# A fused Fourier and retention layer on one core: retention products, operand sums and gate buffers around the folded Fourier projection in another order

## The reference

```python
h_x = modulate(rms_norm(x, norm1_gain), sh1, sc1)            # sh1, sc1, g1, ... from silu(c) @ w_ada + b_ada
u, q, k, v, g, ga, gb = split(h_x @ w_in)                    # u is 512 wide: the Fourier branch
o      = bidirectional_retention(rope(q), rope(k), v)        # 8 heads of 64, chunks of 128
y_four = real(fft2(u over tokens and 128 channels, ortho)) @ four_w_out
y_ret  = (silu(g) * group_norm(o) * gn_gain) @ ret_w_out
y      = sigmoid(ga) * y_four + sigmoid(gb) * y_ret
x      = x + g1 * (y @ w_out)
x      = x + g2 * (square(relu(modulate(rms_norm(x)) @ w_mlp1)) @ w_mlp2)
out    = rms_norm(x) * final_gain
```

## Time and profile before

| | us |
|---|---|
| median of 3 runs (1300.51 to 1301.29) | 1301.24 |
| the profiled execution, its own time | 1299.87 |
| its span, first to last instruction | 1298.1 |
| PE busy | 1257.0 (97%) |
| DVE busy | 888.1 (68%) |
| ACT busy | 610.9 (47%) |
| POOL busy | 156.6 (12%) |

### The profile page before, as it was taken

How to read it: one execution, slowest core, us unless ns; L and a number is a source line. 1 busy time by engine, 2 the same in 40 slices (tenths; PEclk the granted TensorE clock), 3 DMA queues, 4 the chain that set the end, 5 groups by cost and what they waited for, 6 DMA issues and landing times.

```text
span 1298.1 us, 16931 instructions
## 1 busy us (share of the span) xinstructions
PE 1257.0 (97%) x6216; PEld 1037.9 (80%) x6216; DVE 888.1 (68%) x1392; ACT 610.9 (47%) x1038; POOL 156.6 (12%) x99
## 2 busy tenths in 40 slices
PE   6999999996999899999999999999999999999997
PEld 3788788885988688888888888888888888888886
DVE  5572587747556988878588766655646669868966
ACT  7761211244234443442668655555555433554544
POOL 0125420142141000015530000000000000000000
PEclk9999999998999899999999999999999999999999
DMA  9414220112157355567841544444438996468534
GB/s 368 170 33 154 81 91 2 33 23 94 44 175 253 122 198 201 210 250 271 325 160 66 194 152 160 151 160 141 162 114 283 315 287 211 161 220 266 191 101 163
DMA packets 95226, 219.18 MB, mean 169 GB/s; under 512 B 11532, under 2 KB 11932, under 8 KB 95144
## 3 DMA queue, kind: packets, MB, share of 16 engines
q1 hardware_dynamic: 84480, 188.99, 42.5%
q10 hardware_dynamic: 8872, 22.81, 4.8%
q0 software_dynamic: 1792, 6.29, 1.4%
HBM read 166.66 MB, written 51.39 MB: 168 GB/s over the span
## 4 chain that ended last, share of the span: by engine, by line
PE 62%; DVE 2%; issue 1%; DMA 0%; ACT 0%; ACTq 0%; DVEq 0%
PE ps L2975 9%; PE ps L2977 9%; PE ps L2976 9%; PE ps L3576 8%; PE ps L3584 8%; PE ps L3579 8%; PE ps L3602 3%; PE ps L3414 3%; PE ps L3416 3%; PE ps L3419 3%; PE ps L3058 0%; PE ps L3487 0%; PE ps L3481 0%; PE ps L3480 0%; DMA ada_next<-in_ada_columns 0%
## 5 line engine op out<-in xcount | busy, mean ns | idle before, releaser
L2975 PE MATMUL ps<-t_hi,s_hi 128*128 128x512 f32 x392 | 153.3, 391 | 0.0
L2976 PE MATMUL ps<-t_lo,s_hi 128*128 128x512 f32 x392 | 153.0, 390 | 0.0
L2977 PE MATMUL ps<-t_hi,s_lo 128*128 128x512 f32 x392 | 152.9, 390 | 0.0
L1049 POOL TENSOR_TENSOR ring_lo<-raw,ring_hi 128x1024 fp32r<-128x1024 f32 (+2 forms) x37 | 86.8, 2354 | 370.7 <-ACT ring_hi L1170 349.7
L1780 ACT ACTIVATE s_hi<-s_raw 128x512 fp32r<-128x512 f32 x112 | 70.5, 630 | 115.0 <-DMA b<-in_w_stream 60.0
L2854 DVE TENSOR_TENSOR s_lo<-s_raw,s_hi 128x512 fp32r<-128x512 f32 x112 | 77.4, 691 | 43.4 <-ACT s_hi L1780 42.8
L2975 PE MATMUL ps<-ring_hi,hT_hi 128*128 128x512 f32 x224 | 91.2, 407 | 0.0
L2977 PE MATMUL ps<-ring_hi,hT_lo 128*128 128x512 f32 x224 | 87.5, 391 | 0.0
L2976 PE MATMUL ps<-ring_lo,hT_hi 128*128 128x512 f32 x224 | 87.4, 390 | 0.0
L2977 PEld LDWEIGHTS ps<-t_hi,s_lo 128*128 128x128 f32 x392 | 73.7, 188 | 16.0
L2975 PEld LDWEIGHTS ps<-t_hi,s_hi 128*128 128x128 f32 x392 | 73.6, 188 | 16.0 <-DVE t_lo L2858 0.4
(11 more groups left out here) (508 smaller groups left out, 3208.5 us busy)
## 6 DMA issues: line engine op xcount, KB each, us to landing
s_raw<-ff_scr SPq DMA_DIRECT2D x112, 256.0 KB, 2.9
raw<-in_w_stream SPq DMA_DIRECT2D x34, 512.0 KB, 4.3
ff_scr<-ffs SPq DMA_DIRECT2D x16, 1024.0 KB, 4.8
t_raw<-in_w_stream SPq DMA_DIRECT2D x64, 256.0 KB, 3.3
w_B_raw<-in_w_stream SPq DMA_DIRECT2D x48, 256.0 KB, 2.9
ff_scr<-ffa SPq DMA_DIRECT2D x16, 768.0 KB, 4.5
b<-in_w_stream SPq DMA_DIRECT2D x48, 256.0 KB, 4.1
ada_next<-in_ada_columns SPq DMA_DIRECT2D x15, 512.0 KB, 4.1
```

The source lines that it names most:

```text
L1049: nc.gpsimd.tensor_tensor(lo_ap[:, w], raw_of(i)[:, w], hi_ap[:, w].bitcast(F32), ALU.subtract).then_inc(split, 1)
L2975: M(dst, lhsT=l_hi, rhs=r_hi, start=first, stop=False, skip_group_check=goes_on)
L2976: M(dst, lhsT=l_hi, rhs=r_lo, start=False, stop=False, skip_group_check=goes_on)
L2977: return M(dst, lhsT=l_lo, rhs=r_hi, start=False, stop=last, skip_group_check=goes_on)
```

## The change

It alters order, buffer places and semaphore counts; no instruction that computes is added or removed.

- PE: `fold(2)` moves from ahead of product 0 to behind product 1, `fold(3)` from behind product 1 to behind product 2; the row is now fold(0), fold(1) in the g tiles, then products 0, 1, fold(2), 2, fold(3), 3, 4, even projection, 5, 6, odd projection, 7. Five products instead of four lie ahead of the even projection, one instead of two behind the odd one.
- `STREAM`: chunk `re 1` goes ahead of `u 2` and `u 3`. With that, the ring slot of chunk `cs 3` is the one of `re 1`, released by product 7, and `fo 1` has the one of `u 3`.
- DVE: both `second_sum` additions move into loop step j = 14 (needing `h_whole` 6); first sums, operands, `u_lo` and `xq` stand in another order, `xq` ahead of the lo parts.
- ACT: the hi parts and bank copies follow the new order; `cs 3` is split behind the copy of product 7.
- `four_product(0)` does its B part last, and Fourier product m uses banks 3 to 5 for even m and 0 to 2 for odd m (before: the reverse).
- Gates: `g1` and `g2` trade places, as do `ada_late` and `sig7` with their neighbours; DVE's wait for the last three `yf_out` stores goes from ahead of `g1_raw` to ahead of `g2_raw`; lo parts of `B11` go ahead of those of `T3`, `g1_lo` and `g3_lo` go later.

```diff
-          + [("g", i) for i in range(4)] + [("u", 0), ("u", 1), ("re", 0), ("u", 2), ("u", 3), ("re", 1)]
+          + [("g", i) for i in range(4)] + [("u", 0), ("u", 1), ("re", 0), ("re", 1), ("u", 2), ("u", 3)]
...
-        g1_raw = place("g1_raw", o_kv + 8192, [P, 4, 512])
+        g1_raw = place("g1_raw", o_v + 8192, [P, 4, 512])
...
             whole(7)
-            pool.wait_ge(split, INDEX[("re", 1)])
-            for i in range(INDEX[("re", 1)], INDEX[("fo", 0)]):
+            lo(INDEX[("re", 1)])
+            pool.wait_ge(split, INDEX[("cs", 0)])
+            for i in range(INDEX[("cs", 0)], INDEX[("cs", 3)]):
                 lo(i)
             pool.wait_ge(f_used, 10)
             nc.gpsimd.memset(wn_raw[:], 0.0).then_inc(cleared, 1)
-            for i in range(INDEX[("fo", 0)], INDEX[("fo", 2)]):
+            for i in range(INDEX[("cs", 3)], INDEX[("fo", 2)]):
                 lo(i)
...
+                if j == 14:
+                    dve.wait_ge(h_whole, 6)
+                    half_sums(0, ALU.add, 1)
+                    half_sums(1, ALU.add, 1)
...
-                if j in (16, 17):
-                    ret_product(j - 16)
...
-                if j in (15, 17):
-                    fold(2 + (j - 15) // 2)
-
-            for r in (2, 3):
-                ret_product(r)
+                if j == 16:
+                    ret_product(0)
+
+            ret_product(1)
+            fold(2)
+            ret_product(2)
+            fold(3)
+            ret_product(3)
+            ret_product(4)
...
-            for r in (4, 5):
+            for r in (5, 6):
                 ret_product(r)
             pe.wait_ge(f_hi, 8)
             parts(4, slice(HD, P), ((1, 0), (1, 1), (0, 0), (0, 1)))
-            for r in (6, 7):
-                ret_product(r)
+            ret_product(7)
...
             def four_product(m):
                 w_hi, w_lo = chunk(("fo", m // 2))
-                b, ms_ = 3 * (m % 2), slice(m * P, (m + 1) * P)
+                b, ms_ = 3 * (1 - m % 2), slice(m * P, (m + 1) * P)
...
                 elif m == 0:
-                    pe.wait_ge(dft_lo, 10)
-                for n in range(2):
-                    mm3(ps[:, b + 2, :], w_hi[:, w[2 + n]], w_lo[:, w[2 + n]], b_hi[:, n, :], b_lo[:, n, :], n == 0, n == 1)
+                    pe.wait_ge(dft_lo, 9)
+                if m:
+                    b_part(m, b + 2, w)
...
+                if m == 0:
+                    pe.wait_ge(dft_lo, 10)
+                    mm = b_part(m, b + 2, w)
+                mm.then_inc(merge_done, 1)
...
-            for m in range(KT - 3, KT):
-                yf_stored(dve, m)
...
             g_sums(0, ("T3", "T1"))
+            for m in range(KT - 3, KT):
+                yf_stored(dve, m)
             do.chain(V.tensor_tensor(g2_raw[:], g1_raw[:], block(h_raw, 0, 0), ALU.subtract), s_sum)
```

More of the change, by code:

```diff
@@ L125 @@
              ("B22", 1), ("T2", 0), ("T2", 1), ("T4", 0), ("T4", 1)]
-FIRST_LOS = [("T3", 0), ("B11", 0), ("T3", 1), ("B11", 1), ("B21", 0), ("B21", 1), ("T2", 0), ("T1", 0), ("T2", 1),
+FIRST_LOS = [("B11", 0), ("B11", 1), ("T3", 0), ("T3", 1), ("B21", 0), ("B21", 1), ("T2", 0), ("T1", 0), ("T2", 1),
              ("T1", 1), ("B22", 0), ("T4", 0), ("B22", 1), ("T4", 1)]
@@ L330, in program @@
         ada_next = place("ada_next", o_qt + 12288, [P, D])
-        ada_late = [place(f"ada_late{n}", o_kv + 4096 * n, [P, D]) for n in range(3)] + [ada_next]
+        ada_late = [place(f"ada_late{n}", o_v + 4096 * n, [P, D]) for n in range(3)] + [ada_next]
         late_place = [0, 1, 2, 3, 0, 1, 2, 3, 0, 1, 2, 0, 1, 0]
@@ L2183, in split_side, with quarters, half_sums @@
                 ins_.then_inc(side_free[SIDX[key] % 2], 1)
+            def quarters(ks):
+                return h_raw[:, ks, 1:256], h_raw[:, ks, 1023:768:-1], h_raw[:, ks, 511:256:-1], h_raw[:, ks, 513:768]
+            def half_sums(half, op, n):
+                ks = slice(4 * half, 4 * half + 4)
+                x0, x1, x2_, x3 = quarters(ks)
+                if n:
+                    do(V.tensor_tensor(second_sum[:, ks, 1:256], x2_, x3, op))
+                else:
+                    do(V.tensor_tensor(first_sum[:, ks, 1:256], x0, x1, op))
             for j in range(1, 18):
@@ L2515, in _ @@
             g_s_lo("g2", g2_lo[:], g2_raw[:], g2_hi[:], s2_ready)
+            g_s_lo("g3", block(hT_lo, 0, 1), a21_raw, block(hT_hi, 0, 1), s3_ready)
             lo_again(1, 1)
@@ L3350, in turn_gate, with b_part @@
                 nc.tensor.transpose(ps[0:KT, 2 - 2 * a, 0:P], gate_cols[:, a, :], ident[:]).then_inc(gate_turned, 1)
+            def b_part(m, bank, w):
+                w_hi, w_lo = chunk(("fo", m // 2))
+                for n in range(2):
+                    mm = mm3(ps[:, bank, :], w_hi[:, w[2 + n]], w_lo[:, w[2 + n]], b_hi[:, n, :], b_lo[:, n, :], n == 0, n == 1)
+                return mm
             def four_product(m):
                 w_hi, w_lo = chunk(("fo", m // 2))
-                b, ms_ = 3 * (m % 2), slice(m * P, (m + 1) * P)
+                b, ms_ = 3 * (1 - m % 2), slice(m * P, (m + 1) * P)
                 w = [slice((4 * (m % 2) + n) * P, (4 * (m % 2) + n + 1) * P) for n in range(4)]
```

97 lines of the change are left out of this document (44 added, 53 removed).

## The result

The kernel after takes 1280.74 us (median of 4 runs, 1279.04 to 1282.5), against 1301.26 us for the kernel before on the same chip: 20.5 us less, ratio 0.984, 95% interval 0.983 to 0.986. The profiled execution took 1279.04 us, its span is 1277.2. The same kernel measured again on another chip, further down, gave 1282.27 against 1299.73: ratio 0.987, interval 0.985 to 0.988, 17.5 us less.

The account below looks back on a forecast made before the run. PE was busy 97% of the span; the changed stretch was taken as bound by DVE in three pieces. Their gains, 12.5 + 3.0 + 3.0 = 18.5 us, take the median from 1301.24 to 1282.7 us, range 1280 to 1289.

Parts of the forecast that it names:

- the forecast case: Whole kernel: the gains of the three pieces add, 16.5 to 20 us less; chance 52%.
- DVE's three pieces: Stretches bound by DVE: ahead of the even projection, behind the transform, from last Fourier output to gate product 3; 18.5 us.
- Piece 1: Up to the even projection: covered second sums, earlier start, fifth product ahead and fuller clock gain 12.5 us, ends 10 and 14.
- Odd projection: Six DVE operations (7.2 us) stay hidden behind the even projection's rest and two products; product 7 just hides `pa_lo`.
- Piece 2: Behind the transform: A parts need only `ao_lo`, PE stands about 1.1 us; gain 3.0 us, ends 0 and 3.5.
- DVE's row behind `wn_raw`: Behind the odd projection: DVE's splits start at 5.8 us when `wn_raw` lands and end with `ao_lo` at 11.8.
- the risk sat on ACT: Behind the transform: A_odd and B queue behind `fo 1` on ACT; each us of later landing goes to PE in full.
- Piece 3: Gates: `g1_raw` starts without the store wait, gate product 3 is released at 447.0 instead of 450.28; gain 3.0, ends 1 and 4.
- The new gaps cost clock: Rival: half clock behind the transform's gap or in the even projection, or late `fo 1`; gain 13 to 16 us; 26%.
- POOL and SP become the bound: Rival ahead of the even projection: late `re 1` split delays `u 3` load, fold and split; gain 9 to 12.5 us; 8%.
- More than 20 us: Rival: collisions fall out well and the gates' gap is short; gain above 20 us, ceiling 29; 8%.
- Slower: Rival: `fo 1`, ahead of A_odd and B on ACT, lands some 24 us behind its issue; 1304 us or more; 3%.

Follow-up runs that it names:

- the gates alone: Kernel before with only the gates changed (g1 and g2 trade buffers, store wait behind g_raw, order of sums and splits): 1297.38 us against 1300.69, ratio 0.998.

## Why the prediction was right, and where it was not

Predicted were 1282.7 us, 1280 to 1289; measured 1280.74 and, on another chip, 1282.27. The mechanism of the forecast case, DVE's three pieces shortened and adding up, is what happened, and each piece alone was shown to be worth its share. Its size, 16.5 to 20 us less, fits the second measurement (17.5) and the traces (20.1 and 19.4 from the first fold on); the first measurement's 20.5 falls just into the rival case above it. Piece by piece, by the table (predicted gain, measured gain of the kernel after):

- **Piece 1** (12.5 predicted, with 13.0 up to the transform before the 0.5 taken off; 15.3 measured). Right: the two sums (4.3 us, ends 288.3 by this profile's clock, 289.2 by before's) with `u_lo(1)` slipping 0.2; product 0 bound by POOL's `re 0` (292.48, or 293.3 by before's clock); the fifth product 2.7; the projection 14.2 us long at full clock (311.64 to 325.89). The step that failed is this one: "The `split_side(6)` that started at 300.07 waits for the transposes behind product 0; it starts at 297.9 and ends at 299.0." That was the order before (transposes at 298.26, behind product 0). The change also moves product 0 behind these transposes in its loop step, which I had not read from the diff, and PE does them while product 0 waits for POOL, at no cost. So the split ended at 295.8, the projection started at 311.6 instead of 314.8 (312.5 by before's clock: 2.3 earlier than predicted), and the gap ahead of product 2, for which I took off 0.5, did not exist. The run with the order that I had counted brought back the split at 298.0, a gap of 2.0 us ahead of product 2, and a start at 315.4, 0.1 us beyond my range.
- **The price of the sums' cover and of the fifth product** came out as counted: 2.3 us and 2.7 us with a slow start of 1.5, when undone.
- **Odd projection**: hidden, as predicted. PE waited for nothing around it.
- **Piece 2** (3.0 predicted; 2.0 and 2.2 measured). The stall is 2.1 us, not 1.1. The failed step is "At 2.9 us to landing it is there at 9.5, its hi part is done at 10.6, and A_odd and B, which stand behind it on ACT, are just on time": the hi part is done 11.5 us behind the odd projection, because POOL's lo part of `cs 3` met DVE's of `wn`, 1.1 us that I had not counted. And the term that I took as the bound, DVE's row behind `wn_raw` ("11.8"), was not: `wn_raw` was there at 4.0 and not at 5.8, its first operation took 0.7 us and not 1.6, and DVE was through at 9.7 and stood 2.3 us for A_odd. That the risk sat on ACT was right, and moving one line took 1.3 us of it away. The forecast's clock was right: full in both measurements, though at half in one variant with the same gap.
- **Piece 3** (3.0 predicted; 1.9 in the gates and 0.8 behind them in the first measurement, 2.8 and −0.7 in the second, 3.1 in the gates alone). `g1_raw` starts without a wait, and the single gap of 4.0 us at gate product 3 is there. The failed step is "loaded behind 402.66 with 5.1 us to landing: 407.8 instead of 411.14". Against PE's product 8 that is 8.5 us; it was 9.9 in the first measurement, and by these 1.4 us the release came later than forecast. Two terms make them up. The load is issued behind the last two stores of `yf_out` and DVE's row block before, and DVE's last wait for a store grew from 2.53 to 3.34 us; so the issue came 0.8 us later against product 8 (385.30). And row block 2 began 5.8 us behind the issue, not 5.1. `g1_raw`, which starts 0.9 us late, does not matter, since DVE stands 1.57 us for the load behind it; the 0.4 us that B21 was to have in hand became a wait of 0.7. In the second measurement (5.3 us behind the issue) row block 2 started at 9.1 us, and that wait did not come.
- **The rivals.** "The new gaps cost clock" did not happen in either measurement of this kernel, but that may have been luck: the same gap did cost 1.6 us in the run with the sums moved back. "POOL and SP become the bound" did not happen: the only wait in that chain is 0.6 us for `u_lo(2)`. "More than 20 us", to which I gave 8%, is met by the first measurement alone, and there by 0.5 us. "Slower" would have needed a landing of `fo 1` 20 us late; it was 1 us late.

In sum piece 1 was 2.3 to 2.8 us too small, pieces 2 and 3 together 1.3 too large in the first measurement, and 0.8 us of the first profile's span was start-up: 18.5 + 2.8 − 1.3 + 0.8 = 20.8, against 20.8 between the two profiled executions. In the second measurement it is 15.2 for piece 1, 4.3 for the rest, and 1.3 us of later start-up: 18.2 us between the spans. So a part of how near the forecast came is that errors of opposite sign met.

The Trainium skill (SBUF — State Buffer, section "SBUF: two separate sides") has the lock between such DVE and POOL operations as exclusive. The collisions read here agree: two sums took 4.30 us where 2.4 is their own time, and a first sum 2.90 and 3.40. The single first sums ended 1.1 us behind POOL's operation and the two sums 2.2 us behind it, and that operation took no longer than alone (2.36 to 2.39 us). The 288.5 us that my prediction gave for a fair sharing has no working; shared half and half from 285.0, both would end near 289.4. So the end of the two sums, 289.2, does not tell the two rules apart, but POOL's unchanged times do. The same section should have been applied to `cs 3` and `wn` too, the collision that I missed.

## What to carry to other kernels

Before costing a moved instruction, write down what stands directly ahead of it and behind it inside its own loop step: a group of transposes of 0.6 us on one side or the other of a product that waits was worth 3 us here. A load's hi part on an in-order engine belongs behind the copies that the next product needs, even if it looks "just on time"; ahead of them it cost 1.3 us up to product 8. And when the critical engine gets faster, ask of every store and load whether it now ends last: here gate product 3 hung on the load of one row block, and its issue hung on a store for which DVE waited 0.8 us longer than before.
